# Stage 3 of a three-stage layer kernel as one pipeline over all passes, with bounded logarithm arguments

## The chip, the core and the metric

The kernel runs on one core of one Trainium2 chip. The metric is the device time of one execution in microseconds (us), the median of the runs. TensorE (PE) multiplies matrices, VectorE (DVE), ScalarE (ACT) and GpSimd (POOL) work elementwise, and SyncE (SP) issues all the DMAs named here. SBUF is the on-chip memory with 128 partitions; PSUM holds what PE writes, in 8 banks of 128 x 512 float32 (f32).

## The reference, cut to what matters

Two blocks follow each other on a sequence of 2048 tokens of width 1024. The first is a gated linear attention block (stage 1 of the kernel). The second projects its input to the operands of three branches and multiplies their gated outputs by w_out. Its linear recurrence and its sliding window are computed in stage 2. Its third branch, "stick-breaking" attention with 4 heads of 64, is computed in stage 3 together with w_out, the norm and the residual:

```python
z = jnp.einsum('bhqd,bhsd->bhqs', qb, kh) * (S_DH ** -0.5)
strict = kpos[None, :] < tpos[:, None]
log_keep = jnp.where(strict, jax.nn.log_sigmoid(-z), 0.0)
suffix = lax.cumsum(log_keep, axis=3, reverse=True) - log_keep
a = jnp.where(strict, jnp.exp(jax.nn.log_sigmoid(z) + suffix), 0.0)
out = jnp.einsum('bhqs,bhsd->bhqd', a, vh)
...
y = jnp.concatenate([y_m, y_a, y_s], axis=-1) @ w_out
return x + gate[:, None] * rmsnorm_2(y, g_post)
```

Each query needs, for each earlier key, the sum of softplus(z) over the keys between them. The gates silu(z) = z / (1 + exp(-z)) are formed with exponential and logarithm only.

## The kernel before

Stages 1 and 2 walk over 16 tiles of 128 tokens (stage 2 by `all_tiles`, L949). Large products take three matmuls each, since f32 operands are split into a bf16 high and low part (L1413 to L1415). In stage 2 ScalarE forms 1/(1+exp(-z)) as Exp, Ln(1+.), Exp: `gate_out` (L1142) copies a PSUM bank out and writes its Exp beside it, L1210 and L1211 finish the gates of a tile, L1183 to L1185 do the same after the convolution. After these ScalarE makes the high part of the next tile's activations (L1140), VectorE the low part (L1257), and on that TensorE's first matmul of the next tile waits.

Stage 3 is `stick_phase` (L1602). Eight passes of 256 queries; a pass over queries I handles the key blocks I, I-1, ... 0. The work of 128 keys x 2 heads x 256 queries, one 128 x 512 array, is a unit; a pass over I has 4(I+1) units, and all have 144. The passes run in the order I = 0, 7, 1, 6, 2, 5, 3, 4 (`PAIRS`), so in 4, 32, 8, 28, 12, 24, 16 and 20 units. The four units of the largest key block are diagonal: part of them lies on or past the query.

A unit g goes through:

- `scores` (PE L1942, 4 matmuls): z into a PSUM bank Z;
- `z_abs`, `exp_ln` (ACT L1785, L1789, L1791): ln(1+exp(-|z|)) into `ab`;
- `z_copy` (DVE L1856, on the diagonal L1853 with a minimum): z into `zs`;
- `softplus` (DVE L1864, on the diagonal also the mask L1869): `sp_` = max(z,0) + `ab`;
- hi (POOL L1774): the bf16 high part of `sp_`; `low` (DVE L1875): the rest;
- `sums` (PE L1955, L1956, L1959, L1960): running sums over keys by triangular matrices, kept up in PSUM bank C; the first two of a pass leave out two of the four matmuls;
- `exponent` (DVE L1880): z minus the sum; `weight` (ACT L1795): its Exp; `values` (PE L1968): product with v, gathered in PSUM bank O over the pass (cleared by L2000).

`run_units` (L1665) writes each engine's order by hand: in step s an engine does each of its operations for unit s minus that operation's lag. VectorE's order is exponent (lag 3), z_copy (0), low (1), softplus (0). A pass drains before the next one fills.

At the end of a pass `gate` (L1882) multiplies O by a gate and splits the result into high and low parts (`ys_hi` on ACT L1799, L1891). The w_out product of the pass, 4 results k of 8 blocks b of 3 matmuls (`y_product`, L1972), is spread over the steps of the next pass; `y_out` (ACT, L1801) copies each result and takes its squares, `y_scale` (DVE L1902, L1905) scales it and adds the residual, SP stores it. The last pass has its w_out product behind it.

## Time and profile before

| | |
|---|---|
| time, median of 3 | 2326.86 us (2325.99 to 3398.17) |
| profiled execution, its own time | 2321.77 us |
| its span, first to last instruction | 2320.0 us |
| stage 3, from its first matmul | 1778.9 to 2320.0 us |
| busy over the span: PE / DVE / ACT / POOL | 2118.8 / 1422.6 / 1111.8 / 567.5 us |
| mean granted clock of PE | 0.968 of full speed |

The page gives busy times over the whole span, and these are averages over three stages with different limits. Views by stretch give the busy time of each engine in one stage. In lists in order of time a row is: start in us, duration in us, engine, line, operation, output and inputs, count; in brackets the idle time of the engine ahead of it and what ended it. Matmuls overlap, so PE's pace is read from start to start. DVE and ACT rows overlap by up to 0.1 us in the same way.

### The profile page before, as it was taken

To read this page: it belongs to the slowest core of one execution; us is meant where nothing else is said; L and a number is where in the kernel's file an instruction comes from. 1 tells how busy PE (TensorE), PEld (TensorE's weight loads), DVE (VectorE), ACT (ScalarE), POOL (GpSimd) and SP (SyncE) were. 2 spreads that over 40 slices of the span, in tenths; PEclk is the share of its full clock that TensorE was granted. 3 is DMA by queue.
4 is the path that set the end of the run, shared out by engine and by line. 5 is a ranking of instruction groups with operands and counts; after the bars stand their busy time and mean duration, and the time that the engine had idled before them with its cause. 6 is when DMAs were issued, how large, how long until landed. Compare 5 with 4: busy or idle time off the path is not lost. (4 is left out here: it accounts for less than half of the span.)

```text
span 2320.0 us, 48214 instructions
## 1 busy us (share of the span) xinstructions
PE 2118.8 (91%) x19996; PEld 1488.3 (64%) x19996; DVE 1422.6 (61%) x2478; ACT 1111.8 (48%) x2407; POOL 567.5 (24%) x554
## 2 busy tenths in 40 slices
PE   1699999999999998699999999999994698989887
PEld 1466666666666664599988999998992343434333
DVE  6755555555555553256665555666554798989885
ACT  2444444444444443234434334434333687978775
POOL 0520100000000100333343333344332232323221
PEclk9799999999999998899999999999996899999999
DMA  9422222223222224411001011001004312020111
GB/s 398 151 89 81 84 80 76 88 90 102 81 89 85 89 71 141 131 26 46 27 27 30 27 29 46 27 27 30 27 18 155 109 46 82 23 88 19 64 55 55
DMA packets 129962, 174.54 MB, mean 75 GB/s; under 512 B 46928, under 2 KB 98256, under 8 KB 127696
## 3 DMA queue, kind: packets, MB, share of 16 engines
q1 hardware_dynamic: 129456, 170.41, 22.8%
q8 instruction: 158, 2.59, 0.5%
q10 hardware_dynamic: 288, 1.05, 0.1%
q14 instruction: 60, 0.49, 0.1%
HBM read 122.39 MB, written 49.03 MB: 74 GB/s over the span
## 5 line engine op out<-in xcount | busy, mean ns | idle before, releaser
L1413 PE MATMUL m_bank<-h_hi,w_all 128*128 128x128 bf16 (+1 forms) x2560 | 437.5, 220 | 19.2 <-POOL m_arena L1041 17.7
L1415 PE MATMUL m_bank<-h_hi,w_all 128*128 128x128 bf16 (+1 forms) x2560 | 436.9, 220 | 0.1
L1414 PE MATMUL m_bank<-h_lo,w_all 128*128 128x128 bf16 (+1 forms) x2560 | 436.9, 220 | 0.0
L1413 PEld LDWEIGHTS m_bank<-h_hi,w_all 128*128 128x128 bf16 (+1 forms) x2560 | 251.5, 98 | 27.8 <-POOL m_arena L1041 18.2
L1414 PEld LDWEIGHTS m_bank<-h_lo,w_all 128*128 128x128 bf16 (+1 forms) x2560 | 251.7, 98 | 0.6 <-issue 0.2
L1415 PEld LDWEIGHTS m_bank<-h_hi,w_all 128*128 128x128 bf16 (+1 forms) x2560 | 251.7, 98 | 0.0
L1774 POOL TENSOR_TENSOR s_hi<-s_sp,s_cols 128x512 bf16<-128x512 f32 x144 | 152.3, 1057 | 352.9 <-DVE s_sp L1869 141.2
L283 POOL TENSOR_TENSOR g_stage<-g_stage,g_nh_row 128x1024 f32<-128x1024 f32 x16 | 52.3, 3272 | 736.0 <-DVE g_stage L617 736.0
L680 PE MATMUL g_bank<-w_all,h_hi 128*128 128x512 bf16 x512 | 194.2, 379 | 0.7 <-ACT g_stage L372 0.7
L681 PE MATMUL g_bank<-w_all,h_hi 128*128 128x512 bf16 x512 | 194.0, 379 | 0.0
L682 PE MATMUL g_bank<-w_all,h_lo 128*128 128x512 bf16 x512 | 194.0, 379 | 0.0
L680 PE MATMUL g_bank<-h_hi,w_all 128*128 128x128 bf16 x1024 | 175.3, 220 | 0.0
L681 PE MATMUL g_bank<-h_lo,w_all 128*128 128x128 bf16 x1024 | 175.1, 220 | 0.0
L682 PE MATMUL g_bank<-h_hi,w_all 128*128 128x128 bf16 x1024 | 175.0, 220 | 0.0
L1795 ACT ACTIVATE s_ar<-s_ar 128x512 f32<-128x512 f32 x144 | 89.6, 622 | 69.7 <-DVE s_ar L1880 69.6
L1942 PE MATMUL s_bank<-s_q,s_k_c 128*128 128x256 bf16 x576 | 89.6, 281 | 26.9 <-issue 13.7
L1880 DVE TENSOR_TENSOR s_ar<-s_zs,s_bank 128x512 f32<-128x512 f32 x144 | 98.4, 683 | 24.1 <-PE s_bank L1960 22.1
L1968 PE MATMUL s_bank<-s_ar,s_v_c 128*64 128x256 f32 x576 | 94.8, 408 | 14.0 <-ACT s_ar L1795 13.3
L1875 DVE TENSOR_TENSOR s_lo<-s_sp,s_hi 128x512 bf16<-128x512 f32 x144 | 99.2, 689 | 12.9 <-POOL s_hi L1774 12.9
L1791 ACT ACTIVATE s_ab<-s_ab,s_cols 128x512 f32<-128x512 f32 x144 | 104.2, 723 | 4.7
L680 PEld LDWEIGHTS g_bank<-h_hi,w_all 128*128 128x128 bf16 x1024 | 100.8, 98 | 1.8 <-issue 0.2
L1864 DVE SCALAR_TENSOR_TENSOR s_sp<-s_zs,s_ab 128x512 f32<-128x512 f32 x144 | 98.8, 686 | 3.7 <-ACT s_ab L1791 1.4
(349 smaller groups left out, 5295.8 us busy)
## 6 DMA issues: line engine op xcount, KB each, us to landing
g_piece<-in_w_dram SPq DMA_DIRECT2D x64, 268.0 KB, 3.3
g_stage<-in_gla_w_in_dram SPq DMA_DIRECT2D x8, 1552.0 KB, 12.4
g_stage<-in_ada_w_dram SPq DMA_DIRECT2D x8, 1536.0 KB, 11.3
g_piece<-in_w_mod_t_dram SPq DMA_DIRECT2D x48, 256.0 KB, 3.2
w_hi<-g_piece_hi SPq DMA_DIRECT2D x64, 134.0 KB, 2.0
w_lo<-g_piece_lo SPq DMA_DIRECT2D x64, 134.0 KB, 2.2
g_xs<-in_x_dram SPq DMA_DIRECT2D x16, 512.0 KB, 4.3
s_xr<-x SPq DMA_DIRECT2D x16, 512.0 KB, 4.1
```

The lines of the kernel that those rows point to most:

```text
L680: pe.matmul(out, l_hi, r_hi, start=(k == 0), stop=False)
L681: pe.matmul(out, l_hi, r_lo, start=False, stop=False)
L682: ins = pe.matmul(out, l_lo, r_hi, start=False, stop=(k == n - 1))
L1413: pe.matmul(out, l_hi, r_hi, start=(k == 0), stop=False)
L1414: pe.matmul(out, l_hi, r_lo, start=False, stop=False)
L1415: ins = pe.matmul(out, l_lo, r_hi, start=False, stop=(k == n - 1))
L1774: pool.tensor_tensor(hi[k][:], sp_[k], one_col.broadcast_to([P, 512]), ALU.mult).then_inc(s["hi_done"], 1)
L1791: act.activation(ab[k], ab[k], ACT.Ln, bias=one_col).then_inc(s["ln_done"], 1)
L1864: ins = dve.scalar_tensor_tensor(sp_[k], zs[k][:], 0.0, ab[k], ALU.max, ALU.add)
L1875: dve.tensor_tensor(lo[k][:], sp_[k], hi[k][:], ALU.subtract).then_inc(s["lo_done"], 1)
L1880: dve.tensor_tensor(ar[k][:], zs[k][:], C[k % 2][:], ALU.subtract).then_inc(s["arg_done"], 1)
L1968: ins = pe.matmul(O[j * SD:(j + 1) * SD, k % 2 * T2:(k % 2 + 1) * T2], v_h, ar[k][:, j * T2:(j + 1) * T2], start=False, stop=True, skip_gr ...
```

## The change

Stage 3 becomes one pipeline over all 144 units. Passes run in ascending length, I = 0 to 7, and nothing drains between them: 150 steps in all. The lags are now softplus 1, low 2, sums 4, exponent 4, weight 4, values 6, and VectorE's order in a step is exponent, low, z_copy, softplus; on the diagonal z_copy stands ahead of low. Buffers `zs`, `hi`, `lo` go from 4 to 6, Z has 3 banks instead of 4, and the freed bank gives the w_out product two banks M. O is no longer cleared by a matmul of its own.

The diagonal mask moves into the minimum of z_copy (cap at a large negative number), which drops the 32 multiplications L1869; on the diagonal ScalarE now reads the capped copy and so waits for it.

The w_out blocks are dealt out by a table `y_at`: none in steps 0 to 5 and 9 to 11, two in 107 steps and one in 34 (worked out from the loop shown). The last pass has 6 of its 8 blocks in the loop as well; their sum is kept in `y_part`, and 8 blocks are left behind the loop. A finished result is scaled on VectorE 4 steps later (`y_scale`, behind softplus), but the residual is now added by GpSimd, one half per step (`y_add`, behind hi), except in the last pass. SP loads in another order: a second q and two more key blocks first, then the rest; `rows`, the product of the two scale rows, stands in VectorE's step 6.

In stages 1 and 2 each exp(-z) becomes Relu(z+40) and then Exp(40 - that): one more ScalarE pass over the gates (128 x 1024) and one over the convolution result (128 x 384) in each tile of stage 2, and one over 128 x 1024 once in stage 1.

```diff
-                act.activation(e_sb[0:n, at[0]:at[1]], bank[0:n, 0:at[1] - at[0]], ACT.Exp, scale=-1.0)\
+                act.activation(e_sb[0:n, at[0]:at[1]], bank[0:n, 0:at[1] - at[0]], ACT.Relu, bias=floor_col)\
                    .then_inc(s[name + "_read"], 1)
 
...
-                link.done(act.activation(ec, cv, ACT.Exp, scale=-1.0))
+                link.done(act.activation(ec, cv, ACT.Relu, bias=floor_col))
+                link.done(act.activation(ec, ec, ACT.Exp, scale=-1.0, bias=floor_col))
                 link.done(act.activation(ec, ec, ACT.Ln, bias=one_col))
                 act.activation(ec, ec, ACT.Exp, scale=-1.0).then_inc(s["conv_exp"], 1)
...
-        zs = [sb(f"zs{n}", [P, 512]) for n in range(UNITS)]
+        NH = 6
...
+        NZ = 3
+        Z, C, O, M = banks[0:3], banks[3:5], banks[5], banks[6:8]
...
+        SOFT, LOW, SUMS, WEIGHT, VALUES = 1, 2, 4, 4, 6
+        STEPS = NU + VALUES
...
+        def gate_step(n):
+            return BASE[n + 1] + VALUES
...
+        START = 6
+        y_at = {}
+        at = 0
+        for step in range(START, STEPS):
+            room = (len(blocks) * (step + 1 - START)) // (STEPS - START) + 1
+            n_here = 0
+            while at < len(blocks) and at < room + 8 and n_here < 2:
+                n, k, b = blocks[at]
+                if b >= EARLY and n < LAST and step < gate_step(n) + 2:
+                    break
+                if n_here == 1 and at >= room:
+                    break
+                y_at.setdefault(step, []).append(blocks[at])
+                at += 1
+                n_here += 1
+        tail_blocks = blocks[at:]
+
+        def y_end(step):
+            return [(n, k) for n, k, b in y_at.get(step, []) if b == (NY if n < LAST else EARLY) - 1]
 
...
+            load_kv("kv_in", 0, 2)
             load_q(0)
+            load_q(1)
+            load_kv("kv_near", 2, 6)
             load_yz(0)
-            weights()
-            for n in range(NP2):
+            for dst, src in ((wo_hi, w2_hi), (wo_lo, w2_lo)):
+                sp.dma_start(dst[:], src[:, NIN:NIN + D].rearrange("(k p) n -> p k n", p=P)).then_inc(s["wo_in"], 16)
+            load_yz(1)
+            load_kv("kv_rest", 6, NT)
+            for dst, src in ((g_row[:], gate_d), (gp_row[:], g_post[0])):
+                sp.dma_start(dst, src.partition_broadcast(P)).then_inc(s["consts_in"], 16)
+            load_x(0)
+            load_x(1)
+            for n in range(1, NP2):
...
             pool.memset(cols[:, 42:43], 0.0).then_inc(s["consts_ready"], 1)
 
-            for g in range(BASE[NP2]):
-                k = g % UNITS
-                pool.wait_ge(s["sp_done"], g + 1)
-                wait("cs_done", g - 1)
-                pool.tensor_tensor(hi[k][:], sp_[k], one_col.broadcast_to([P, 512]), ALU.mult).then_inc(s["hi_done"], 1)
+            def y_add(n, tt, h):
+                half = slice(h * 512, (h + 1) * 512)
+                pool.wait_ge(s["x_in"], 32 * (n + 1))
+                pool.wait_ge(s["y_scaled"], 4 * n + 2 * tt + h + 1)
+                pool.tensor_tensor(xr[n % 2][:, tt, half], xr[n % 2][:, tt, half], y_sb[:, 2 * tt + h, :], ALU.add)\
+                    .then_inc(s["y_used"], 1)
+
+            for step in range(STEPS + 6):
+                g, k = step - SOFT, (step - SOFT) % UNITS
+                if 0 <= g < NU:
+                    pool.wait_ge(s["sp_done"], g + 1)
+                    wait("cs_done", g - NH + 3)
+                    pool.tensor_tensor(hi[g % NH][:], sp_[k], one_col.broadcast_to([P, 512]), ALU.mult).then_inc(s["hi_done"], 1)
+                for h in range(2):
+                    for n, k in y_end(step - 4 - h):
+                        if n < LAST and k % 2 == 1:
+                            y_add(n, k // 2, h)
 
...
+            def z_abs_exp_ln(g):
+                k = g % UNITS
                 wait("sp_done", g - 3)
-                act.activation(ab[k], Z[k][:], ACT.Abs).then_inc(s["abs_done"], 1)
-
-            def exp_ln(g, k, diagonal, pair):
+                if unit(g)[3]:
+                    act.wait_ge(s["z_read"], g + 1)
+                    act.activation(ab[k], zs[g % NH][:], ACT.Abs).then_inc(s["abs_done"], 1)
...
+            def z_copy(g):
+                n, u, k, diagonal, pair = unit(g)
+                wait("arg_done", g - NH + 1)
...
-                    ins.then_inc(s["masked"], 1)
-                    masked[0] += 1
-                    dve.wait_ge(s["masked"], masked[0])
-                    ins = dve.tensor_tensor(heads2(sp_[k]), heads2(sp_[k]),
-                                            keep[:, k // 2:k // 2 + 1, :].broadcast_to([P, 2, T2]), ALU.mult)
-                ins.then_inc(s["sp_done"], 1)
...
+            def ys_low(n):
+                side = n % SIDES
                 dve.wait_ge(s["ys_hi_done"], n + 1)
-                dve.tensor_tensor(ys_lo[:].rearrange("p b t -> p (b t)"), ys, ys_hi[:].rearrange("p b t -> p (b t)"),
-                                  ALU.subtract).then_inc(s["ys_lo_done"], 1)
+                dve.tensor_tensor(ys_lo[side][:].rearrange("p b t -> p (b t)"), ys,
...
+                dve.wait_ge(s["y_done"], UNITS * (LAST + 1) + k + 1)
+                wait("y_used", 4 * (LAST - 1) + k + 1)
+                dve.wait_ge(s["part_read"], k + 1)
+                dve.tensor_tensor(y_sb[:, k, :], M[k % 2][:], y_part[:, k, :], ALU.add).then_inc(s["y_read"], 1)
...
 
                 dve.wait_ge(s["row_done"], 1)
-                dve.wait_ge(s["x_in"], 32 * (n + 1))
                 dve.wait_ge(s["y_stat"], 2 * n + tt + 1)
                 for h in range(2):
                     half = slice(h * 512, (h + 1) * 512)
                     yt = y_sb[:, 2 * tt + h, :]
                     dve.scalar_tensor_tensor(yt, yt, rsy[:, tt:tt + 1], gp_row[:, half], ALU.mult, ALU.mult)\
                        .then_inc(s["y_scaled"], 1)
-                    dve.wait_ge(s["y_scaled"], 4 * n + 2 * tt + h + 1)
-                    dve.tensor_tensor(xr[:, tt, half], xr[:, tt, half], yt, ALU.add).then_inc(s["y_used"], 1)
-
...
+            for step in range(STEPS):
+                for n in range(LAST):
+                    if step == gate_step(n):
+                        gate(n)
+                if 0 <= step - SUMS < NU:
+                    exponent(step - SUMS)
+                if step < NU and unit(step)[3]:
+                    z_copy(step)
+                if 0 <= step - LOW < NU:
+                    low(step - LOW)
+                for n in range(LAST):
+                    if step == gate_step(n):
+                        ys_low(n)
+                if step < NU and not unit(step)[3]:
+                    z_copy(step)
+                if 0 <= step - SOFT < NU:
+                    softplus(step - SOFT)
+                if step == START:
                     rows()
-            gate(NP2 - 1)
-            y_scale(NP2 - 2, 1)
+                for n, k in y_end(step - 4):
+                    if n < LAST and k % 2 == 1:
+                        y_scale(n, k // 2)
...
+            ys_low(LAST)
+            for late in range(STEPS, STEPS + 4):
+                for n, k in y_end(late - 4):
+                    if n < LAST and k % 2 == 1:
...
+                y_whole(2 * tt)
+                y_whole(2 * tt + 1)
+            for tt in range(2):
+                y_scale(LAST, tt)
...
+            def y_early(n, k, b):
+                if b == 0:
+                    if n == 0 and k == 0:
+                        pe.wait_ge(s["wo_in"], 32)
+                    if k == 0:
+                        pe.wait_ge(yz_in[n % SIDES], 96 * (n // SIDES + 1))
+                    done = UNITS * n + k - 1
+                    wait("y_read", min(done, UNITS * LAST))
+                    wait("part_read", done - UNITS * LAST)
+                y_product(n, k, b, b == 0, b == (NY if n < LAST else EARLY) - 1)
+
+            scores(0)
+            for step in range(STEPS):
+                if 0 <= step - SUMS < NU:
+                    sums(step - SUMS)
+                if 0 <= step - VALUES < NU:
+                    values(step - VALUES)
+                for n, k, b in y_at.get(step, []):
+                    y_early(n, k, b)
+                if step + 1 < NU:
+                    scores(step + 1)
+            for n, k, b in tail_blocks:
+                y_early(n, k, b)
+            for k in range(UNITS):
+                if k < 2:
+                    pe.wait_ge(s["part_read"], UNITS - 1 + k)
+                else:
+                    pe.wait_ge(s["y_read"], UNITS * LAST + k - 1)
+                for b in range(EARLY, NY):
```

## Rows read from the trace of the kernel before

**Rows 1.** Windows: us busy per engine, clock, DMA: stage 2, stage 3, loading.

```profile
core 0: us, PE busy (x) PEld busy (x) DVE busy (x) ACT busy (x) POOL busy (x), PEclk, DMA share, GB/s
1600.00:1700.00 100.00, 99.91 (x1344) 90.77 (x1342) 59.56 (x118) 41.06 (x119) 38.21 (x38) 1.00 0.10 26
...
1811.47:2288.04 476.57, 433.61 (x2332) 191.35 (x2333) 417.38 (x655) 386.44 (x693) 148.11 (x140) 0.97 0.16 52
...
1795.00:1800.00 5.00, 2.57 (x16) 0.71 (x12) 1.13 (x2) 1.26 (x2) 0.00 (x0) 0.98 1.05 388
```

**Rows 2.** PE, timeline, stage 3: one step with two w_out blocks.

```profile
2274.51 0.60 PE L1942 MATMUL s_bank<-s_q,s_k_c 128*128 128x256 bf16 x4
2275.04 0.65 PE L1968 MATMUL s_bank<-s_ar,s_v_c 128*64 128x256 f32 x4
...
2276.50 0.38 PE L1989 MATMUL s_bank<-s_wo_hi,s_ya 128*128 128x512 bf16 x1
...
2277.80 0.60 PE L1942 MATMUL s_bank<-s_q,s_k_c 128*128 128x256 bf16 x4
```

**Rows 3.** PE, timeline, stage 3: first sums of a pass.

```profile
1954.01 0.61 PE L1959 MATMUL s_bank<-s_hi,s_tri 128*128 128x512 bf16 x1 [5.13 <-DVE s_lo L1875]
```

**Rows 4.** DVE, timeline, stage 3: softplus, low, softplus.

```profile
1867.87 0.68 DVE L1864 SCALAR_TENSOR_TENSOR s_sp<-s_zs,s_ab 128x512 f32<-128x512 f32 x1
...
1869.71 0.69 DVE L1875 TENSOR_TENSOR s_lo<-s_sp,s_hi 128x512 bf16<-128x512 f32 x1
1870.32 0.68 DVE L1864 SCALAR_TENSOR_TENSOR s_sp<-s_zs,s_ab 128x512 f32<-128x512 f32 x1
```

**Rows 5.** POOL, timeline, stage 3: a plain hi, one beside y_scale.

```profile
1868.64 1.04 POOL L1774 TENSOR_TENSOR s_hi<-s_sp,s_cols 128x512 bf16<-128x512 f32 x1 [4.41 <-DVE s_sp L1864]
...
2193.96 1.38 POOL L1774 TENSOR_TENSOR s_hi<-s_sp,s_cols 128x512 bf16<-128x512 f32 x1 [2.24 <-PE s_bank L1960]
```

**Rows 6.** DVE, timeline, stage 3: y_scale beside the second hi.

```profile
2193.76 0.69 DVE L1905 TENSOR_TENSOR s_xr<-s_xr,s_y_sb 128x512 f32<-128x512 f32 x1
2194.37 1.53 DVE L1902 SCALAR_TENSOR_TENSOR s_y_sb<-s_y_sb,s_cols,s_gp_row 128x512 f32<-128x512 f32 x1
```

**Rows 7.** ACT, timeline, stage 3: one unit's pace, then one y_out.

```profile
1868.60 0.72 ACT L1791 ACTIVATE s_ab<-s_ab,s_cols 128x512 f32<-128x512 f32 x1
...
1871.03 0.72 ACT L1791 ACTIVATE s_ab<-s_ab,s_cols 128x512 f32<-128x512 f32 x1
...
1921.20 0.58 ACT L1805 ACTIVATE s_y_sb<-s_bank 128x512 f32<-128x512 f32 x1
...
1923.00 0.58 ACT L1785 ACTIVATE s_ab<-s_bank 128x512 f32<-128x512 f32 x1
```

**Rows 8.** DVE, timeline, start of stage 3: scale rows, second pass.

```profile
1810.33 1.23 DVE L1843 TENSOR_TENSOR s_gp_row<-s_gp_row,s_g_row 128x1024 f32<-128x1024 f32 x1 [13.27 <-DMA s_gp_row<-in_g_post_dram]
...
1813.86 0.69 DVE L1853 TENSOR_TENSOR s_zs<-s_bank,s_cap 128x512 f32<-128x512 f32 x1 [0.32 <-ACT s_ab L1785]
```

**Rows 9.** DVE and SP, timeline, end: last gate, last store.

```profile
2288.04 0.69 DVE L1888 TENSOR_TENSOR s_ys<-s_bank,s_sz 128x512 f32<-128x512 f32 x1 [1.42 <-PE s_bank L1968]
...
2316.39 0.34 SPq L1722 DMA_DIRECT2D out_dram<-s_xr  x1
```

**Rows 10.** ACT, DVE, PE, timeline, stage 2: gates to next tile.

```profile
1391.35 1.15 ACT L1210 ACTIVATE m_arena<-m_arena,m_cols 128x1024 f32<-128x1024 f32 x1
...
1394.20 0.39 ACT L1214 ACTIVATE m_arena<-m_bank 128x256 f32<-128x256 f32 x1 [0.61 <-PE m_bank L1415]
...
1395.56 1.54 DVE L1257 TENSOR_TENSOR h_lo<-m_arena,h_hi 128x1024 bf16<-128x1024 f32 x1 [4.93 <-ACT h_hi L1140]
...
1397.49 0.23 PE L1413 MATMUL m_bank<-h_hi,w_all 128*36 128x128 bf16 x1
```

**Rows 11.** POOL, timeline, stage 2: product of two f32 arrays.

```profile
1393.66 2.36 POOL L1118 TENSOR_TENSOR m_arena<-m_arena 128x1024 f32<-128x1024 f32 x1 [5.55 <-ACT m_arena L1211]
```

**Rows 12.** Instruction groups, ACT: table load of stage 3.

```profile
L1779 ACT ACT_TABLE_LOAD x1 | 1.3, 1283 | 11.7 <-PEq L56 11.7
```

More of the change, by code:

```diff
@@ L28 @@
 TAU = 16.0
+FLOOR = 40.0
 GA = 32
@@ L1209, in tile @@
                 act.wait_ge(s["sz_read"], i + 1)
+                link.done(act.activation(e_sb, e_sb, ACT.Exp, scale=-1.0, bias=floor_col))
                 link.done(act.activation(e_sb, e_sb, ACT.Ln, bias=one_col))
@@ L1741, in _ @@
+            for n in range(NP2 - 3, NP2):
+                store(n)
+                if n == NP2 - 3:
+                    sp.wait_ge(s["x_out"], 32 * (n + 1))
+                    load_x(NP2 - 1)
+            sp.wait_ge(s["x_out"], 32 * NP2)
         @block.gpsimd
@@ L1818, in y_out @@
+                    wait("y_scaled", 4 * (n - 1) + 2 * (tt + 1))
                     act.activation(rsy[:, tt:tt + 1], lny[:, tt:tt + 1], ACT.Exp, scale=-0.5).then_inc(s["y_stat"], 1)
[L1820 to L1831 removed]
@@ L1903, in y_scale @@
                        .then_inc(s["y_scaled"], 1)
-                    dve.wait_ge(s["y_scaled"], 4 * n + 2 * tt + h + 1)
-                    dve.tensor_tensor(xr[:, tt, half], xr[:, tt, half], yt, ALU.add).then_inc(s["y_used"], 1)
-            def y_scales(n):
-                def beside(step):
-                    if step == min(y_ready(n, 1) + 2, COUNT[n] - 1):
-                        y_scale(n - 1, 0)
-                return beside
-            stages = [(exponent, 3), (z_copy, 0), (low, 1), (softplus, 0)]
@@ L1914, in _ @@
-            for n in range(NP2):
-                if n > 0:
-                    gate(n - 1)
-                if n > 1:
-                    y_scale(n - 2, 1)
-                run_units(n, stages, y_scales(n) if n > 0 else None)
-                if n == 0:
-                    rows()
-            gate(NP2 - 1)
-            y_scale(NP2 - 2, 1)
+                    if n == LAST:
+                        dve.wait_ge(s["x_in"], 32 * (n + 1))
+                        dve.wait_ge(s["y_scaled"], 4 * n + 2 * tt + h + 1)
+                        dve.tensor_tensor(xr[n % 2][:, tt, half], xr[n % 2][:, tt, half], yt, ALU.add).then_inc(s["y_last"], 1)
@@ L2006, in _ @@
[L2006 to L2015 removed]
+                    y_hi, y_lo = (v[side][:, b - EARLY, ts] for v in (ys_hi, ys_lo))
@@ new lines, in y_product @@
+                pe.matmul(bank[:], y_hi, wo_hi[:, b, cs], start=first, stop=False)
+                pe.matmul(bank[:], y_hi, wo_lo[:, b, cs], start=False, stop=False)
+                ins = pe.matmul(bank[:], y_lo, wo_hi[:, b, cs], start=False, stop=last)
+                if last:
+                    ins.then_inc(s["y_done"], 1)
+            def y_early(n, k, b):
[8 more added lines that the diff above has]
+                y_product(n, k, b, b == 0, b == (NY if n < LAST else EARLY) - 1)
```

318 lines of the change are left out of this document (149 added, 169 removed).

## The prediction

> **What bounds the kernel now.** I read the windows of busy time first, then the order of time of each engine in a step of stage 3, then what ended the idle time. Stages 1 and 2 are TensorE's: in a stretch of stage 2 it is busy for 99.91 of 100 us at full clock, ScalarE for 41 [rows 1]. Only stage 3 leaves something. Between its first and last gate 476.6 us go by [rows 1, 9]. In that stretch lie 140 units and 224 w_out blocks. A unit takes TensorE 0.53 for the scores and 1.46 for values and sums, so 1.99 us; a block takes 1.30/2 = 0.65 [rows 2]. That gives 140 x 1.99 + 224 x 0.65, less 14 units with half the sums (1.30/6 = 0.22 per matmul, so 0.43 each): 278.6 + 145.6 - 6.0 = 418 us. The other 58 us are lost, mostly at the seven pass boundaries: the first sums of a pass come after 5.13 us of idle TensorE, and the first of them then takes 0.61 us [rows 3] instead of the 0.38 us of a matmul of the same size in a full step [rows 2], at the lower clock level. The mean granted clock of the stretch is 0.97 [rows 1]. Ahead of the stretch VectorE waits 13.27 us for the scale rows [rows 8], and behind it 32 us go to the last w_out product and the store.
>
> **The change part by part.** The sum is made against the profiled span, 2320.0 us (time 2321.8; the median of the runs, 2326.9, lies 5 us above).
>
> *Stages 1 and 2.* In a tile ScalarE forms the gates 6.1 us ahead of TensorE's next tile: gates, copy, high part, low part, first matmul. The low part starts at 1395.56 and takes 1.54, so it ends 0.39 us before that matmul [rows 10]. The new Exp over 128 x 1024 is priced at L1210's 1.15 us. ScalarE has 0.61 us idle behind the gates, waiting for TensorE, so the low part comes 0.5 us later and TensorE 0.1 to 0.2: 15 tiles, 2 us, and 1 us for the exposed last tile and stage 1. The Exp over the convolution, about 0.6, lies under TensorE's wait-free products. Bounds: 0 (the slack holds) and 15 x 0.8 = 12 us (nothing of 1.15 but the slack is hidden). I take +3.
>
> *Start.* The scale rows were ready at 1810.3 [rows 8]. Ahead of them in SP's queue now also stand a second q (4 x 128 KB) and a second set of y operands and gates (1.04 MB), 1.57 MB at 388 GB/s [rows 1] = 4.0 us. So `rows`, in VectorE's step 6, ends at 1814.3 + 1.2 = 1815.5. By then VectorE has done six steps (they fit between 1780.7 and 1797) and stands still, and all engines with it. Before, the second pass began at 1813.9 with an empty pipeline [rows 8].
>
> *The step of VectorE.* This is where I expect the gain to go. Softplus of unit s-1 is the last operation of step s; low of that unit is the second of the next. Between them lies GpSimd's hi: softplus starts at 1867.87, hi runs from 1868.64 for 1.04 us, low starts at 1869.71, 1.84 us after softplus [rows 4, 5]. Before, exponent and z_copy filled this gap and softplus followed low by 0.61, a step of 2.45 us. Now z_copy stands behind low, and the gap holds one operation: 1.84 + 0.61 + 0.61 = 3.06 us. On the diagonal z_copy is ahead of low and the step stays 2.45. TensorE's mean from step 31 on, with 204 blocks in 119 steps, is 1.99 + 1.71 x 0.65 = 3.10. The two engines are level before anything is added.
>
> *y_scale and y_add.* VectorE and GpSimd stop each other. Beside a hi that took 1.38 instead of 1.04 us, the y_scale issued at 2194.37 took 1.53, where the add ahead of it took 0.69: it waited until hi ended at 2195.34 and ran 0.56 more [rows 5, 6]. Of 144 hi only six are longer than 1.04, all beside L1902 or L1905, whose inputs lie in SBUF. An operation that waits goes ahead of the next one in the other queue. Softplus and low too take both inputs from SBUF; now GpSimd runs two adds more per y_scale. One add over 128 x 512: half of 2.36 for 128 x 1024, 1.18 us [rows 11]; bounds 1.04 [rows 5] and 2.36. In a step with y_scale, from softplus on: the first half runs at 0.61, hi gets in at 1.2 and ends at 2.24, the second half ends at 2.8, the add gets in behind it until 3.98, low ends at 4.54 instead of 2.40: +2.0 us (2.1 less an overlap). In the next step the second add starts behind low at 2.4 and holds softplus back from 3.06 to 3.58: +0.5. Together 2.5 us for each of 14 y_scales. Bounds: 0.7 if nothing collides (two halves of about 0.65, in part in the gap of hi), 3.2 if the second add gets in ahead of low, and 4.9 with an add of 2.36. I take 2.5, the value from the nearest rows.
>
> The Trainium skill says the same in its page SBUF — State Buffer, section "Who interferes with whom": a VectorE instruction with two SBUF inputs and a GpSimd instruction that reads SBUF exclude each other, whoever is first. It is what makes me extend two pairs of rows to softplus and low, which no row here shows beside GpSimd; without it the extra would lie between 0.7 and 2.5.
>
> *Sum of VectorE's path*, steps 7 to 143: 112 plain steps x 3.06 = 342.7; 25 diagonal steps x 2.45 = 61.3; 14 x 2.5 = 35.0; seven `ys_low` x 0.61 = 4.3 (gate itself lies in the gap of hi). On the diagonal ScalarE waits for z_copy and can't run ahead; its unit takes 2.43 and a y result 1.80 [rows 7], so four diagonal units with one result take 11.5 against 9.8: after 1 us of slack 0.7 for each pass, 4 us. Cold clock and TensorE-bound early steps with two blocks (3.29 us [rows 2]): 3. Sum 450.3, so step 144 begins at 2265.8. The mask L1869 (32 x 0.69) is gone from VectorE, but in steps where it hid nothing of TensorE's; it is in the 2.45 already.
>
> *Drain.* Low of the last unit 1.9 + 1.8 us later, its sums, then five TensorE steps without scores, the last values at +9.7: the last gate at 2275.5 instead of 2288.0 [rows 9].
>
> *End.* Gate, high, low take 2.1 us as before. Then only 8 blocks: 1.3 us each pair with `y_whole` (0.7) behind, four times one after the other, to +8.2. Square, norm and y_scale of the second half end at +13.9, and the last store goes out; it took from 2316.39 to 2320.0 [rows 9]. That is 17.6 us behind the gate against 32.0.
>
> Span: 2275.5 + 17.6 + 3 = 2296, 24 us less than before. The median: **2303 us**, 1.0% less.
>
> **The rivals.**
>
> *TensorE bounds the pipeline.* Nothing collides, an event costs 0.7, VectorE's path falls by 25 us under TensorE's. From step 12 (three steps of 3.06 without blocks and one at the start lie before it, so from 1829 on): 136 units x 1.99, less 12 x 0.43 and 5 scores already done, plus 2 values, 264; 242 blocks x 0.65 = 157; cold clock and gates 5. Last gate 2255, span 2255 + 17.6 + 3 = 2276, median 2283. For it: VectorE and ScalarE have slack buffers of more than a step towards TensorE, and in the old long passes TensorE held its pace. Against it: [rows 5, 6]. It decides if an event costs under about 1 us.
>
> *The collisions are worse.* The second add gets ahead of low (+0.7 x 14 = 10) or an add takes 2.36 (+33): median 2313 to 2336.
>
> *The tables of ScalarE.* Relu is new. If it needs a table of its own, each Relu and the Exp behind it load one, 1.28 us each [rows 12]. The place is the sz gate, right ahead of the high part of the next tile: 2 x 1.28 + 0.5 = 3.1 us late against 0.39 of slack, 2.7 x 15 = 40 us. Median 2343, slower than before. It decides as soon as one such load stands in a tile. For it: nothing but that no Relu occurs before. Against it: Copy, Square, Abs, Identity, Exp and Ln already share the one load of each stage. The Trainium skill (ScalarE: Activation LUTs, section "Table sets: the hidden batching unit") says that relu is in every set; by that the 40 us are none. No run here shows it yet.
>
> *The pipeline brings nothing*: the waits of the boundaries come back as waits of values for the gate, since one bank O remains. The seven gates lie in VectorE's gap of 1.84 us and TensorE runs up to a step ahead; even 3 us each give +21, median 2324.
>
> **How the numbers follow.** Forecast (2290 to 2313) 0.47; TensorE-bound (2272 to 2290) 0.30; worse collisions, or gates (2313 to 2336) 0.15; tables 0.03; anything else 0.05. The range 2276 to 2322 leaves out the lower end of the second case, the upper half of the third and the tables, 0.2 in all. About 2% is what a measurement of this kernel can tell from no change, so the marks are 2280 and 2373: below lie half of the second case and some of the rest, 0.18 in all; above 0.03. Within 2% is left with 0.79.
>
> **What would show it.** Right: plain steps of 3.05 to 3.1 us on VectorE with idle time ahead of low put down to hi; softplus or y_scale rows of 1.1 us and more beside y_add; no matmul of stage 3 at the lower clock after the start; `rows` at about 1814 + 3; last gate at about 2278; three table loads in all. Wrong: steps alternating 3.29 and 2.63 on TensorE without waits (the first rival); y_add far from 1.2 us; TensorE idle ahead of the first matmul of stage 2's tiles by more than 0.3 us.

## The result, and the profile after

The changed kernel takes 2333.14 us (median; 2330.93 to 2337.29), the kernel before 2325.94 us on the same chip. The ratio is 1.0035, 95% interval 1.0026 to 1.0045: a little slower, where 1.0% faster was forecast, and outside the forecast range of 2276 to 2322.

| | before | after | forecast |
|---|---|---|---|
| span of the profiled execution | 2320.0 | 2330.3 | 2296 |
| first matmul of stage 2 | 951.7 | 955.2 | |
| first load of stage 3 (SP) | 1772.0 | 1795.5 | about 1775 |
| `rows` begins | 1810.3 | 1835.7 | 1814.3, before the shift |
| last gate | 2288.0 | 2312.5 | 2275.5, before the shift |
| last gate to the end | 32.0 | 17.8 | 17.6 |

Stage 3, from its first matmul to the end of the span, did become shorter: 541.1 us before (1778.87 to 2320.0), 528.1 after (1802.21 to 2330.3). Stage 2 took more than that away: 820.3 us before, 840.4 after.

Windows of busy time of the kernel after: the stretch of stage 2 that [rows 1] shows, then nearly all of stage 2 and of stage 3.

```profile
core 0: us, PE busy (x) PEld busy (x) DVE busy (x) ACT busy (x) POOL busy (x), PEclk, DMA share, GB/s
1600.00:1700.00 100.00, 97.54 (x1286) 88.27 (x1283) 59.83 (x115) 43.90 (x120) 35.91 (x37) 0.98 0.11 31
...
955.00:1795.00 840.00, 800.49 (x10640) 725.37 (x10640) 482.71 (x919) 356.93 (x971) 309.03 (x316) 0.98 0.11 29
1802.00:2330.00 528.00, 465.49 (x2464) 203.34 (x2464) 426.13 (x633) 402.86 (x728) 196.76 (x172) 0.96 0.22 72
```

Where [rows 1] had 99.91 us of TensorE in 100, there are now 97.54. ScalarE has gained only 2.8 us (41.06 to 43.90), and no engine but TensorE is nearly full. So it is a matter of order, and one tile shows it. Timeline of the kernel after, ScalarE, GpSimd, VectorE and TensorE at the end of a tile (start, duration, in brackets the idle time ahead and what ended it), the counterpart of [rows 10, 11]; the last row is TensorE's first matmul of the next tile:

```profile
1405.54 1.15 ACT L1216 ACTIVATE m_arena<-m_arena,m_cols 128x1024 f32<-128x1024 f32 x1
1406.72 1.15 ACT L1217 ACTIVATE m_arena<-m_arena,m_cols 128x1024 f32<-128x1024 f32 x1
1407.90 1.06 ACT L1218 ACTIVATE m_arena<-m_arena 128x1024 f32<-128x1024 f32 x1
1408.86 0.37 ACT L1221 ACTIVATE m_arena<-m_bank 128x256 f32<-128x256 f32 x1
1409.13 1.05 ACT L1145 ACTIVATE h_hi<-m_arena 128x1024 bf16<-128x1024 f32 x1
...
1409.04 2.35 POOL L1123 TENSOR_TENSOR m_arena<-m_arena 128x1024 f32<-128x1024 f32 x1 [6.82 <-ACT m_arena L1218]
...
1410.21 2.27 DVE L1264 TENSOR_TENSOR h_lo<-m_arena,h_hi 128x1024 bf16<-128x1024 f32 x1 [5.47 <-ACT h_hi L1145]
1412.40 0.55 DVE L1371 TENSOR_TENSOR m_arena<-m_bank,m_cols 128x388 f32<-128x388 f32 x1
...
1412.53 0.23 PE L1420 MATMUL m_bank<-h_hi,w_all 128*36 128x128 bf16 x1 [0.86 <-DVE h_lo L1264]
```

L1216 is the added Exp, 1.15 us. Everything behind it comes later: the high part, and also GpSimd's product of the gates, L1123, which can start only after L1218. That product and the low part L1264 both read SBUF. The low part begins at 1410.21, the product ends at 1411.39, the low part at 1412.48, 1.09 us behind it. Of its 2.27 us, then, it stood still for about half. In the kernel before the same thing stands in [rows 10, 11], small: the product ends at 1396.02, the low part, which has 1.54 us, at 1397.10, 1.08 us behind it.

Groups of stage 2 (955 to 1765), three of the kernel before, then the low part of the kernel after: busy us, mean ns of one, idle time ahead and what ended it.

```profile
L1413 PE MATMUL m_bank<-h_hi,w_all 128*128 128x128 bf16 x2550 | 434.4, 220 | 1.4 <-DVE h_lo L1257 0.7
L1118 POOL TENSOR_TENSOR m_arena<-m_arena 128x1024 f32<-128x1024 f32 x16 | 37.7, 2357 | 88.0 <-ACT m_arena L1211 88.0
L1257 DVE TENSOR_TENSOR h_lo<-m_arena,h_hi 128x1024 bf16<-128x1024 f32 x15 | 23.1, 1543 | 73.9 <-ACT h_hi L1140 73.9
```

```profile
L1264 DVE TENSOR_TENSOR h_lo<-m_arena,h_hi 128x1024 bf16<-128x1024 f32 x15 | 33.9, 2260 | 82.1 <-ACT h_hi L1145 82.1
```

TensorE's waits of after in the same stretch (engine and line, whom it waits for: us in total, times, longest):

```profile
...
PE m_bank L1420 <- DVE h_lo L1264: 14.0, 15, 2.0
PE m_bank L1420 <- ACT m_arena L1170: 5.2, 14, 0.4
```

14.0 + 5.2 = 19.2 us, nearly all of the 20.0 us that stage 2 is longer; before, 0.7 us stood there. L1170 (L1165 before) is ScalarE's copy of the next tile's convolution input out of PSUM. Its row in both kernels, before and after:

```profile
1406.67 0.47 ACT L1165 ACTIVATE m_arena<-m_bank 128x384 f32<-128x384 f32 x1
```

```profile
1422.04 0.47 ACT L1170 ACTIVATE m_arena<-m_bank 128x384 f32<-128x384 f32 x1
```

It starts 9.57 and 9.56 us behind the end of the low part (1397.10 and 1412.48), and it does at 14 of the 15 tiles of both. So these 5.2 us are read as the same lateness, which reaches TensorE a second time: before, TensorE began a tile 0.39 us behind the end of the low part, now it begins at once, and the copy comes later against it by that.

### The profile page after: what moved, and what is told of

Its sections match the earlier page's. It is cut to its first block and busy times, and to the rows that moved or that the text cites. A ratio compares the mean times of both kernels' runs of the same rounds, so it can differ in the third digit from the quotient of the medians.

```text
span 2330.3 us, 48413 instructions
## 1 busy us (share of the span) xinstructions
PE 2121.4 (91%) x19988; PEld 1488.3 (64%) x19988; DVE 1421.1 (61%) x2422; ACT 1143.3 (49%) x2440; POOL 607.7 (26%) x579
## 3 DMA queue, kind: packets, MB, share of 16 engines
q1 hardware_dynamic: 129488, 170.41, 22.6%
## 5 line engine op out<-in xcount | busy, mean ns | idle before, releaser
L1925 DVE TENSOR_TENSOR s_lo<-s_sp,s_hi 128x512 bf16<-128x512 f32 x144 | 118.3, 822 | 47.1 <-POOL s_hi L1810 46.7
L2047 PE MATMUL s_bank<-s_ar,s_v_c 128*64 128x256 f32 x576 | 96.2, 413 | 25.9 <-DVE s_ys L1938 18.6
L1931 DVE TENSOR_TENSOR s_ar<-s_zs,s_bank 128x512 f32<-128x512 f32 x144 | 97.9, 680 | 10.8 <-PE s_bank L2036 10.1
L685 PEld LDWEIGHTS g_bank<-h_lo,w_all 128*128 128x128 bf16 x1024 | 101.0, 99 | 0.1
```

What stands on the lines that cost most here:

```text
L685: pe.matmul(out, l_hi, r_lo, start=False, stop=False)
L1925: dve.tensor_tensor(lo[g % NH][:], sp_[g % UNITS], hi[g % NH][:], ALU.subtract).then_inc(s["lo_done"], 1)
L1931: dve.tensor_tensor(ar[k][:], zs[g % NH][:], C[k % 2][:], ALU.subtract).then_inc(s["arg_done"], 1)
L2047: ins = pe.matmul(O[j * SD:(j + 1) * SD, k % 2 * T2:(k % 2 + 1) * T2], v_h, ar[k][:, j * T2:(j + 1) * T2], start=(u == 0), stop=True, skip ...
```

## The experiments

**One half of the change each.** First the bounded logarithms alone (stages 1 and 2 of after, stage 3 of before), then the new stage 3 alone.

> The kernel before with only the bounded logarithm arguments of stages 1 and 2. Theory 1 (the extra Exp shifts GpSimd's product of the gates by its full 1.15 us, and that product keeps VectorE's low part h_lo waiting, since both read SBUF): TensorE idles 0.86 us ahead of each tile and 0.37 us within it, so about 22 us more than the kernel before, near 2348 us, with h_lo at about 2.26 us instead of 1.54. Rival (the 23 us by which stage 3 began later come from elsewhere, since ScalarE has 59% idle there): the time of the kernel before, near 2326.

Measured: 2343.24 us, ratio 1.0074 (1.0058 to 1.0091), 17.4 us more and not 22. Stage 2 took 840.2 us in its trace, as in the changed kernel, and the low part stands in TensorE's waits with the same 14.0 us; but from the first matmul of stage 3 to `rows` it was 28.5 us instead of 31.5.

> The kernel before with only the new stage 3. Theory 1: the changed kernel less 22 us, near 2311, about 13 us under the kernel before; first matmul of stage 3 at 1779, last gate at 2289. Rival: the two parts of the change are not independent (clock, DMA), and the sum is off by more than 3 us.

Measured: 2316.37 us, ratio 0.9951 (0.9936 to 0.9966), 5 us above the expected 2311. Against 2325.81 before in this comparison, the logarithms cost 17.4 us and stage 3 brings 9.4. The sum, +8.0, is the whole change (+7.2) within the noise: two effects of opposite sign that add.

**The stall in stage 2, from its two ends.** The Exp moved ahead for the columns that are there already:

```
+act.activation(e_sb[:, 0:768], e_sb[:, 0:768], ACT.Exp, scale=-1.0, bias=floor_col)
 gate_out("sz", G0, P, (768, 1024), i, par)
-link.done(act.activation(e_sb, e_sb, ACT.Exp, scale=-1.0, bias=floor_col))
+link.done(act.activation(e_sb[:, 768:1024], e_sb[:, 768:1024], ACT.Exp, ...))
```

> The changed kernel, with one edit in the tiles of stage 2: the gates' first exponential over columns 0 to 767 (read from what is already in SBUF) is put ahead of the last gate's eviction, and only columns 768 to 1023 are left behind it. Of the 1.15 us that the added exponential costs at the place where TensorE waits, 0.31 stay (256 columns; a 128x256 copy is 0.38 us), 0.84 go. Theory A (in stage 2 the time is lost because the whole chain last gate, exponentials, h_hi and GpSimd's product, h_lo is one link later): the idle time of TensorE before a tile's first product falls from 0.86 to about 0.05 us and stage 2 from its first matmul to the first load of stage 3 from 840.4 to about 827; stage 3 unchanged: 2333 - 13 = 2320 us, range 2315 to 2324. Theory B (ScalarE has simply more work in stage 2, wherever it stands, and what it does earlier delays something else): stage 2 stays within 3 us of 840, total 2330 to 2336.

Measured: 2324.87 us, ratio 0.9997 (0.9987 to 1.0006); stage 3's first matmul at 1794.85 instead of 1802.21. The same two waits of TensorE in this kernel:

```profile
...
PE m_bank L1423 <- ACT m_arena L1170: 5.2, 14, 0.4
PE m_bank L1423 <- DVE h_lo L1267: 4.4, 15, 1.3
```

The place of the added work is worth 8.3 us, and the time lies 0.9 us above theory A's range and well below theory B's. Theory A holds, with 9.6 us less of the wait for the low part instead of the 12 expected. The 5.2 us for L1170 stay, though ScalarE's gates come earlier: TensorE still waits for the low part at every tile, and L1170 still stands 9.56 us behind it. Then the product of the gates cut to a column, with ScalarE as in the changed kernel:

```
-pool.tensor_tensor(z_sb[par], z_sb[par], e_sb, ALU.mult)
+pool.tensor_tensor(z_sb[par][:, 0:1], z_sb[par][:, 0:1], e_sb[:, 0:1], ALU.mult)
```

> The changed kernel with GpSimd's product of the gates in stage 2 cut to one column of 1024 (this leaves out the gate's factor in the other 1023 columns). ScalarE's order and its extra exponential stay as they are. Theory A1 (h_lo waits for GpSimd's product, which reads SBUF at the same time and began a link later): h_lo takes 1.2 us instead of 2.26, TensorE's 0.86 us of idle time before each tile goes, stage 2 820 to 826 instead of 840.4, total about 2316 us (2311 to 2320). Theory A2 (h_lo is late because ScalarE's h_hi is late by the added exponential, and GpSimd's product lies beside it by chance): h_lo's mean falls, but TensorE's idle time stays and the total is 2328 to 2336.

Measured: 2316.25 us, ratio 0.9963 (0.9949 to 0.9977); first matmul of stage 3 at 1785.47. TensorE's waits in this kernel, then VectorE's group of the low part:

```profile
...
PE m_bank L1420 <- ACT m_arena L1170: 4.0, 14, 0.3
PE m_bank L1420 <- DVE h_lo L1264: 1.0, 1, 1.0
```

```profile
L1264 DVE TENSOR_TENSOR h_lo<-m_arena,h_hi 128x1024 bf16<-128x1024 f32 x15 | 18.4, 1225 | 82.4 <-ACT h_hi L1145 82.4
```

The low part takes 1.23 us instead of 2.26, TensorE waits once for it instead of 15 times, and 16.9 us come back, though ScalarE still has the added Exp in its old place. So A1 holds: what reached TensorE is the low part standing behind the product. In the kernel before, the same cut:

> The kernel before, with GpSimd's product of the gates in stage 2 cut to one column (this leaves out the gate's factor in the other 1023 columns). In the changed kernel the same cut brought 17 us. Theory A (in the kernel before the product also holds h_lo up, 1.54 instead of 1.2 us, but h_lo is still in time for TensorE, which waits 0.7 us in all of stage 2): within 3 us of 2326. Theory B (the hold-up costs TensorE there too): 4 to 6 us less, 15 x 0.33.

Measured: 2325.83 us, ratio 1.0006 (0.9988 to 1.0024): the times show no cost of the hold-up of 0.3 us in the kernel before, and the 4 to 6 us of theory B are outside the interval. The trace is finer and shows a small one. TensorE's first matmul of two tiles that follow each other, kernel before, then this one:

```profile
1397.49 0.23 PE L1413 MATMUL m_bank<-h_hi,w_all 128*36 128x128 bf16 x1
...
1447.31 0.23 PE L1413 MATMUL m_bank<-h_hi,w_all 128*36 128x128 bf16 x1
```

```profile
1397.69 0.23 PE L1413 MATMUL m_bank<-h_hi,w_all 128*36 128x128 bf16 x1
...
1447.29 0.23 PE L1413 MATMUL m_bank<-h_hi,w_all 128*36 128x128 bf16 x1
```

A tile takes 49.82 us before and 49.60 without the product, and 51.06 to 51.07 in the changed kernel. At the start of a tile the slack hid the hold-up; at L1165 0.2 us of it came through, 3 us over the tiles (TensorE's weight loads of L1413 wait 3.0 us for L1165 in the kernel before). The profiled execution of this run had five short stretches at the lower clock in stage 2 where the kernel before had one, so its span doesn't show the gain either. The 1.15 us of the Exp used the slack up, and the rest went through.

**Stage 3: the copy first.**

```
-if step < NU and unit(step)[3]:
+if step < NU:
     z_copy(step)
 low(step - LOW); ys_low(n)
-if step < NU and not unit(step)[3]:
-    z_copy(step)
```

> The changed kernel with z_copy ahead of low on VectorE in all steps, not only on the diagonal. Theory 2 (a plain step of 3.05 us is softplus to low through GpSimd, 1.84 us, with one operation in the gap, and then three): VectorE's own step falls to 2.45, TensorE becomes the bound with 1.99 us a unit and 0.65 a block, and the loop from the scale rows to the last gate falls from 475.6 to about 440, near 2297 in all. Rival (TensorE or ScalarE already set the pace of the plain steps, which have 3.10 and 2.8 us of work): no more than 5 us gained.

Measured: 2310.51 us, ratio 0.9931 (0.9915 to 0.9948), 22.6 us less than the change, not 36. From the end of `rows` to the last gate it is 451.8 us where 440 were expected. From softplus 7 to softplus 144, the 7th and the last of stage 3, it is 440.1 us instead of 465.7. Of 137 steps only 41 have 2.45 us; 50 lie between 3.2 and 3.93 and 16 between 2.6 and 2.9. VectorE's wait for GpSimd's high part has fallen from 45.0 to 1.1 us; in its place it waits 32.9 us for TensorE's sums (45 times) and 16.2 us for ScalarE's Abs (13 times), and [rows 2] has 3.29 us of TensorE for a step with two blocks. So the placing of the copy was worth more than 20 us, until TensorE and in part ScalarE took over. TensorE itself still waits 16.4 us for the gates in this kernel; whether a second output bank pays here was not tried.

**Stage 3: the residual's sum.** One column of 512 in GpSimd's sum for each half.

> The changed kernel with GpSimd's residual add of all passes but the last cut to one column (the other 511 of each half are left out, the waits stay). Theory 3 (the adds keep low and softplus waiting): the two steps at a y_scale fall from 4.99 and 4.10 us to about 4.5 and 3.05, 14 times, so 21 us less, near 2312; low and softplus are never longer than 0.7. Rival (the extra 3 us at a y_scale are y_scale itself and hi): under 5 us gained.

Measured: 2319.56 us, ratio 0.9969 (0.9955 to 0.9982). An event takes 4.51 + 3.04 us instead of 4.99 + 4.10, as expected; the 14 pairs are 18.3 us shorter. The other steps grew by 6.3, nearly all of it in diagonal steps and in steps at a gate, and 13.6 us are left in the time: the gain is partly given back at the pass boundaries. This kernel leaves out 511 of 512 columns of each sum.

**Stage 3: what holds the gate steps.** The seven steps with an inner gate take 35.0 us where 7 x 3.67 = 25.7 were reckoned, the seven behind them 25.0. The trace names two candidates, TensorE's wait for the gate and VectorE's for ScalarE's high part (kernel after, TensorE's and VectorE's waits from 1836 to 2305):

```profile
PE s_bank L2047 <- DVE s_ys L1938: 18.6, 7, 4.3
...
DVE s_zs L1913 <- ACT s_ab L1830: 6.2, 7, 1.8
DVE s_ys_lo L1944 <- ACT s_ys_hi L1844: 5.9, 5, 2.2
```

A second output bank takes away the first of them. It comes from the score banks, so there is a control with two of those:

```
-NZ = 3
-Z, C, O, M = banks[0:3], banks[3:5], banks[5], banks[6:8]
+NZ = 2
+Z, C, O, M = banks[0:2], banks[3:5], (banks[5], banks[2]), banks[6:8]
-    wait("ys_done", n)
+    wait("ys_done", n - 1)
```

> The changed kernel with two score banks in PSUM instead of three, nothing else: the control for the next kernel. TensorE may then run one unit less ahead of VectorE and ScalarE. If the third bank does nothing, 2333 us; if TensorE needs it, up to 10 us more, 2333 to 2343.

Measured: 2331.89 us, ratio 1.0038 (1.0025 to 1.0051): the third score bank does nothing that can be measured.

> Two score banks, and the bank that is set free takes the outputs of every other pass, so that the first values of a pass no longer wait until VectorE's gate has read those of the pass before. Theory A (the steps around the seven inner gates are long, 4.25 to 5.92 us with 35.0 in all where 25.7 were reckoned, because TensorE stands still for the gate, 18.6 us in seven waits): the waits go and the kernel is 8 to 14 us faster than the control of two score banks and one output bank. Theory B (VectorE's step is bound by low's wait for GpSimd, and TensorE's standing still is slack): 0 to 3 us faster.

Measured: 2332.61 us, ratio 1.0038 (1.0024 to 1.0052). TensorE's wait for the gate is gone, 18 us of it, and nothing is gained in the time (1.5 us in the loop, 465.7 to 464.2); the gate steps take 35.0 us. TensorE now stands 28.8 us for VectorE's copy and 8.0 for ScalarE's Abs instead. The largest wait in the rows was slack. Next the low part of the gated outputs, moved behind softplus (`ys_low`):

> The changed kernel; of a gate's step only the low part of the gated outputs is moved, from behind low to behind softplus, so that VectorE no longer stands there for ScalarE's high part (5.9 us in five waits, 0.5 to 2.2 each) ahead of the copy and of the next softplus. Theory (those waits are on VectorE's path, and make the gate steps longer than reckoned): the seven gate steps shrink by 5 to 6 us in all, total 2326 to 2329. Rival (the step then waits for TensorE or for GpSimd instead): 2331 to 2335.

Measured: 2329.84 us, ratio 1.0021 (1.0011 to 1.0030), between the two ranges. The gate steps fell to 25.3 us, the steps behind them rose to 31.7; 463.3 us for the loop, 2.4 less. Both at once:

> The two edits at the gates together: two score and two output banks, and the low part of the gated outputs behind softplus. Alone the second bank brought nothing (VectorE then waits as before for ScalarE's high part), and the later low part brought 2.4 us in the loop: the seven gate steps fell from 35.0 to 25.3 us, but the steps behind them rose from 25.0 to 31.7. Theory (at each gate VectorE's wait for ScalarE and TensorE's wait for the gate lie beside each other, and taking one away shows the other): together they bring 6 to 9 us in the loop from softplus 7 to softplus 144 (465.7 us in the changed kernel), total 2324 to 2327. Rival (what is behind the gate is bound by something else, the clock or GpSimd): 461 to 464 us in the loop, 2328 to 2332.

Measured: 2327.32 us, ratio 1.0011 (1.0001 to 1.0021), 458.4 us for the loop: 7.3 less, where the edits alone brought 1.5 and 2.4. VectorE's waits in this kernel over the same stretch:

```profile
...
DVE s_zs L1913 <- ACT s_ab L1830: 7.4, 9, 1.8
DVE s_ar L1931 <- PE s_bank L2036: 1.9, 5, 0.7
DVE s_ys_lo L1944 <- ACT s_ys_hi L1844: 1.2, 2, 0.6
```

The line of L1931 behind L2036 has 9.6 us in the changed kernel, 14.1 with `ys_low` alone moved, here 1.9. The two waits lay side by side, and either hid what the other was worth. This rests on one trace each; the times agree in direction (ratios 1.0038, 1.0021 and 1.0011 against 1.0035), but their intervals are too wide to show by themselves that the two edits bring more together than apart.

**Put together.** Early Exp and copy first:

> Both at once on the changed kernel: the exponential over columns 0 to 767 early in stage 2, and in stage 3 the copy of the drained sum ahead of the low part in every step (2310.5 us by itself). If the two places are independent, the gains add: 2310.5 minus what the early exponential alone brings (13 expected), so about 2297 us (2292 to 2303). If stage 3's length depends on when it starts (its loads then meet stage 2's writes), they add to less: 2303 to 2310.

Measured: 2301.94 us, ratio 0.9904 (0.9879 to 0.9929). 8.6 us less than the copy alone, where the early Exp alone brought 8.3: the gains add. With the scale rows at step 14 as well:

> The kernel with both edits (early exponential, copy first), and the rows of the last part (the 16.5 us wait of VectorE for the gp_row transfer, with the work behind it) at step 14 of stage 3 instead of step 6. Theory (VectorE stands still at the start of stage 3 for that transfer while TensorE runs out of drained banks, so the wait is on the path): the wait falls below 4 us, the last gate comes 10 to 15 us earlier, total about 2285 us (2280 to 2291). Rival (the transfers of the first passes bound the start anyway, and TensorE could not have gone on): 2294 to 2300 us.

Measured: 2297.3 us, ratio 0.9875 (0.9857 to 0.9894). VectorE's 17 us wait for the rows is gone, but in its place it waits 8.7 and 4.4 us for TensorE, and only about 5 us are gained: the time is in the rival's range. TensorE's rows and the windows show why (kernel with all three edits; the last two columns of the windows are DMA share and GB/s). TensorE stands for two transfers, and the DMA engines are full until 1830 and nearly so until 1840.

```profile
1816.72 0.61 PE L2065 MATMUL s_bank<-s_wo_hi,s_ym 128*128 128x512 bf16 x1 [7.39 <-DMA s_wo_lo<-w_lo]
...
1837.49 1.03 PE L2022 MATMUL s_bank<-s_q,s_k_c 128*128 128x256 bf16 x4 [4.47 <-DMA s_q<-sq_d]
```

```profile
1800.00:1810.00 10.00, 5.69 (x24) 2.64 (x24) 8.89 (x15) 8.65 (x15) 4.37 (x5) 0.83 1.03 369
1810.00:1820.00 10.00, 3.28 (x12) 1.43 (x13) 2.10 (x4) 3.49 (x6) 1.82 (x2) 0.66 1.07 365
1820.00:1830.00 10.00, 8.50 (x48) 3.67 (x46) 7.80 (x13) 7.58 (x13) 2.28 (x3) 1.00 1.07 380
1830.00:1840.00 10.00, 5.15 (x24) 2.13 (x24) 5.83 (x10) 4.88 (x9) 2.92 (x3) 0.82 0.93 249
```

The residual's sums back on VectorE, and that stage 3 behind stages 1 and 2 of the kernel before; last, the same for the version with the sums on GpSimd:

> The kernel with early exponential, copy first and late rows (2297.3 us), and the residual's sums back on VectorE: one half (scaling and sum) in each of two steps, between the copy and the low part; GpSimd keeps only the high parts. A half is about 0.54 + 0.69 = 1.23 us, so 14 x 2 x 1.23 = 34.4 us of VectorE; in the kernel that it starts from, the same 14 events lengthen the two steps behind them from 2.45..3.28 to 4.51 and 3.51, by about 2.6 us, 36 us in all. Theory A (the price of an event is the waiting for GpSimd's sum, as the thin sum showed with 13.6 us): the two steps become 3.7 each at most, 2288 to 2295 us. Theory B (the sum's time only moves from one engine to the other): 2296 to 2303 us.

Measured: 2301.05 us, ratio 0.9886 (0.9865 to 0.9907), not to be told from 0.9875 with the sums on GpSimd. That is theory B: the sum's time only moves to the other engine.

> Stages 1 and 2 of the kernel before (logarithm arguments not bounded), stage 3 of the kernel just named. Against it only the stall in stage 2 that the early exponential leaves (TensorE waits 4.4 us in all for h_lo and 5.2 for ScalarE's eviction, with the product's 0.7) and the 3 us of stage 1 can go: 8 to 14 us less than that kernel, about 2281 us. If stage 3 gives back what stage 2 gains, because its first transfers then stand nearer to stage 2's writes: 0 to 5 us less.

Measured: 2290.59 us, ratio 0.9839 (0.9824 to 0.9853), 10.5 us less than with the logarithms bounded, inside the 8 to 14 expected.

> Stages 1 and 2 of the kernel before, stage 3 of the changed kernel with the copy first and the rows at step 14 (the residual's sums on GpSimd). With the early exponential in stage 2 this stage 3 took 2297.3 us, and with the sums on VectorE the same exchange of stages 1 and 2 brought 10.5 us (2301.1 to 2290.6): 2287 us, range 2284 to 2291.

Measured: 2285.53 us, ratio 0.9834 (0.9817 to 0.9851). It beats both kernels, and so does the one before it; the two can't be told apart, since the kernel before also took 2322.61 us in this comparison and 2326.92 in the last one. Both give up the bounded logarithms. With them, 2297.3 us is the lowest; 2301.05, with the sums on VectorE, can't be told from it.

## Why the prediction was wrong

The span was put at 2296 and is 2330.3. The 34 us divide as follows.

*Stages 1 and 2: +20.5. This is the step that failed.* I took +3 with bounds of 0 and 12; 23.5 us were measured up to the first load of stage 3, 3.5 of them ahead of stage 2. The slack of 0.39 us between low part and first matmul [rows 10] was right. What I did with it was not. I gave ScalarE 0.61 us of idle time as cover, but the chain that sets the low part's end did not run through ScalarE's idle time alone. It ran from L1211 through GpSimd's product to the low part, and on this chain all of 1.15 us counts. TensorE's first matmul then waited 0.86 us at 14 tiles and 2.0 at the first, 14.0 in all, against 0.76 = 1.15 - 0.39. Even my upper bound, 15 x 0.8, had only that share; the other 5.2 us are TensorE waiting 14 times for L1170, which stands 9.56 us behind the low part and is late with it. The price of this chain was to be seen in my own rows: product 1393.66 to 1396.02 in [rows 11], low part 1.54 us long in [rows 10], where [rows 8] has 1.23 us for a two-input operation of 128 x 1024 on VectorE, and the low part itself takes 1.23 with the product cut. I used that exclusion for stage 3 and did not look for it in stage 2. The Trainium skill's page SBUF — State Buffer, section "Who interferes with whom", which I cited for stage 3, bears on this place as well; the trace agrees with it, by the 1225 ns of the low part with the product cut and 2260 ns beside it.

*Start of stage 3: -2.2.* From the first load to `rows` 40.1 us against 42.3 reckoned: right.

*VectorE's loop: +15.2* (467.4 us from the end of `rows` to softplus 144; 450.3 were reckoned to the beginning of step 144, and softplus 1.9 behind it, so 452.2).

- Plain step 3.06 and diagonal step 2.45: the steps of the loop have 3.05 (70 times) and 2.45 (18 times). Right.
- Event 2.5 (a `y_scale` with its two sums): it is 3.0, for 14 of them +7. What one of the bounds had came true, the second sum getting in ahead of low. VectorE, then GpSimd, in the kernel after:

```profile
2227.80 0.68 DVE L1921 SCALAR_TENSOR_TENSOR s_sp<-s_zs,s_ab 128x512 f32<-128x512 f32 x1
2228.40 0.68 DVE L1931 TENSOR_TENSOR s_ar<-s_zs,s_bank 128x512 f32<-128x512 f32 x1
2229.64 1.73 DVE L1925 TENSOR_TENSOR s_lo<-s_sp,s_hi 128x512 bf16<-128x512 f32 x1 [0.56 <-POOL s_hi L1810]
2231.29 0.68 DVE L1913 COPY s_zs<-s_bank 128x512 f32<-128x512 f32 x1
2231.89 0.68 DVE L1921 SCALAR_TENSOR_TENSOR s_sp<-s_zs,s_ab 128x512 f32<-128x512 f32 x1
2232.49 0.68 DVE L1931 TENSOR_TENSOR s_ar<-s_zs,s_bank 128x512 f32<-128x512 f32 x1
2233.72 0.69 DVE L1925 TENSOR_TENSOR s_lo<-s_sp,s_hi 128x512 bf16<-128x512 f32 x1 [0.56 <-POOL s_hi L1810]
...
2228.56 1.04 POOL L1810 TENSOR_TENSOR s_hi<-s_sp,s_cols 128x512 bf16<-128x512 f32 x1 [1.83 <-DVE s_sp L1921]
2229.56 1.27 POOL L1802 TENSOR_TENSOR s_xr<-s_xr,s_y_sb 128x512 f32<-128x512 f32 x1
2232.65 1.04 POOL L1810 TENSOR_TENSOR s_hi<-s_sp,s_cols 128x512 bf16<-128x512 f32 x1 [1.83 <-DVE s_sp L1921]
```

  From softplus at 2227.80 to softplus at 2231.89 it is 4.09 us; the plain step behind has 3.04. GpSimd has the sum waiting and starts it as hi ends, at 2229.56; low, which waits for the same hi, starts at 2229.64 and takes 1.73 us.
- `ys_low` 0.61 each: +9.3 over the reckoned gate steps, of which about 1 belongs to an event, whose second step is the third gate's. I put down the instruction and not its wait for ScalarE's high part (5.9 us). The rival "pipeline brings nothing" had TensorE's wait for the gate, which is there with 18.6 us and costs nothing by itself. The runs with the edits apart and together account for 7.3 us of the 8.3 that are left.
- The copy waits for Abs in the first steps behind a diagonal block, 6.2 us where I had 4.
- These three come to about 17.5 us; the rest of the loop gave some 2 back.

*Drain and end: +0.4 and +0.2.* 8.2 us from softplus 144 to the last gate against 7.8 (9.7 from the beginning of the step), and 17.8 against 17.6. Right.

Sum: 20.5 - 2.2 + 15.2 + 0.4 + 0.2 = 34.1. One of my signs of being wrong came true, TensorE idle for more than 0.3 us ahead of a tile of stage 2. One sign of being right did not: single stretches of 3.4 us at the lower clock stand in stage 3 too, five between 1847 and 2216 (granted clock 0.50 from 1915.4 to 1918.6, for one). And of the 144 hi before, seven and not six are longer than 1.04 us; the seventh, 1.09, changes nothing.

Of the rivals, TensorE as the bound did not come in the changed kernel, and does for the most part as soon as the copy stands first. The tables fell: three table loads in all and no gap at the gates, as the Trainium skill's page ScalarE: Activation LUTs, section "Table sets: the hidden batching unit", has it for relu. The rival "collisions are worse" had the direction and the mechanism of stage 3.

What stays open: why the other steps took back 6.3 us when the sum was made thin, and about 1 us of the gate steps. That L1170's 5.2 us are the low part's lateness is read from the traces; no edit took this wait away by itself.

## To carry over

Before an instruction is added to a chain with a slack, look at the durations in that chain: one that is longer than its shape takes elsewhere (1.54 for 1.23 us) is already waiting, and the slack is to be measured on the engine that it waits for. A wait in the rows is worth what its neighbours leave of it: taking away 18.6 us of TensorE's waiting brought 1.5 us in the loop, moving what waited 5.9 us on VectorE 2.4, but both together 7.3. When a pipeline is written out, price each operation's place against the gap it was filling: the same copy ahead of low instead of behind it was worth 22.6 us, more than the 9.4 of the whole new stage 3 as it stood.

## What was not expected of the hardware

- A low part of 128 x 1024 takes 1225 ns alone and 2260 ns when GpSimd's product of the same size has started 1.17 us ahead of it, and then ends 1.09 us behind the product. A 128 x 512 sum on GpSimd has 1.27 us where it starts as hi ends, and 1.72 where `y_scale` is still running on VectorE (1493 ns in the mean of 28).
- A sum that waits on GpSimd behind hi starts 0.08 us ahead of VectorE's low, which waits for the same hi: low of 0.69 us became 1.73, at 13 of the 14 events.
- In stage 2, where TensorE is busy for 99.91 of 100 us before and 97.54 after, the granted clock is at the lower level in single short stretches, 3.4 us each, whose number differs between the profiled executions. A tile with such a stretch takes 51.45 us instead of 49.81. The kernel with the new stage 3 alone had five of them, and reached stage 3 at 1787.13, with the same code up to there as the kernel before, which was there at 1778.87 with one: 4 x 1.64 = 6.6 of the 8 us. A difference of 8 us between two single profiles of this kernel need not be the edit's.
